# A router in plain fp32, and a final norm in which the gain is multiplied ahead of the factor

## What is computed

```python
x = x + concatenate([a, r]) @ w_out[l]
h = rmsnorm(x, ffn_norm[l])                   # x / sqrt(mean(x^2) + eps) * gain
logits = h @ w_router                         # 256 x 8
top_logits, top_idx = lax.top_k(logits, 2)
gates = softmax(top_logits)
x = x + sum over the 2 experts e of  gate_e * ((silu(h @ w_gate[e]) * (h @ w_up[e])) @ w_down[e])
return rmsnorm(x, final_norm)
```

## Time and profile before

| what | value |
|---|---|
| median of 3 runs | 1946.05 us (1945.35 to 1947.36) |
| the profiled execution | 1945.6 us, span 1943.3 us |
| TensorE busy | 1894.8 us, 98% of the span |
| VectorE busy | 1499.3 us, 77% |
| ScalarE busy | 1239.7 us, 64% |
| GpSimd busy | 391.1 us, 20% |
| granted TensorE clock, mean | 0.993 of full speed |
| expert stage | from about 976 to 1928 us |

### The profile page before, as it was taken

One profiled execution on the slowest core, in us unless ns is written; L12 is line 12 of the kernel. 1 busy time (PEld: TensorE's weight loads), 2 busy tenths in 40 slices (PEclk: granted clock), 3 DMA queues, 4 the chain that ended last, 5 costly groups with the idle time before them and its releaser, 6 DMA issues.

```text
span 1943.3 us, 27184 instructions
## 1 busy us (share of the span) xinstructions
PE 1894.8 (98%) x9931; PEld 1611.9 (83%) x9931; DVE 1499.3 (77%) x1604; ACT 1239.7 (64%) x1441; POOL 391.1 (20%) x204
## 2 busy tenths in 40 slices
PE   8999999999998999999899999999999999999997
PEld 6788879998887999878688888888888888888885
DVE  7545356666765666696689999999999999899997
ACT  6554444444643444464378888888878888888885
POOL 6756870001823000282340000000000000000000
PEclk9999999999999999999999999999999999999999
DMA  9534556665433667443489999999999999999994
GB/s 277 171 111 131 177 172 207 224 217 163 138 120 108 209 214 227 152 138 124 147 332 394 376 396 378 375 395 354 395 355 397 396 354 395 355 395 396 357 396 177
DMA packets 251401, 524.54 MB, mean 270 GB/s; under 512 B 10008, under 2 KB 58784, under 8 KB 251184
## 3 DMA queue, kind: packets, MB, share of 16 engines
q1 hardware_dynamic: 244000, 506.36, 73.1%
q10 hardware_dynamic: 5088, 10.03, 1.4%
q0 software_dynamic: 2224, 6.96, 1.1%
HBM read 508.12 MB, written 15.20 MB: 269 GB/s over the span
## 4 chain that ended last, share of the span: by engine, by line
PE 89%; DVE 6%; ACT 2%; issue 2%; DMA 0%; POOL 0%; DVEq 0%; SPq 0%; ACTq 0%
PE bank L696 27%; PE bank L698 26%; PE bank L697 26%; PE bank L1048 1%; PE bank L1214 1%; DVE w_lo_sb L1781 1%; PE bank L770 1%; PE bank L743 1%; PE bank L749 1%; ACT w_hi_sb L1351 0%; DVE left_hi_sb L1740 0%; PE bank L1101 0%; ACT w_hi_sb L1371 0%; DVE arena L1736 0%; PE bank L1099 0%
## 5 line engine op out<-in xcount | busy, mean ns | idle before, releaser
L1781 DVE TENSOR_TENSOR w_lo_sb<-arena,w_hi_sb 128x1024 fp32r<-128x1024 f32 x672 | 806.6, 1223 | 74.7 <-ACT w_hi_sb L1351 48.9
L1351 ACT ACTIVATE w_hi_sb<-arena 128x1024 fp32r<-128x1024 f32 x672 | 710.3, 1062 | 165.3 <-PE bank L698 164.7
L696 PE MATMUL bank<-w_hi_sb,left_hi_sb 128*128 128x512 f32 (+1 forms) x1424 | 563.4, 396 | 9.6 <-POOL w_lo_sb L632 3.8
L698 PE MATMUL bank<-w_hi_sb,left_lo_sb 128*128 128x512 f32 (+1 forms) x1424 | 552.2, 388 | 0.0
L697 PE MATMUL bank<-w_lo_sb,left_hi_sb 128*128 128x512 f32 (+1 forms) x1424 | 551.4, 387 | 0.0
L1371 ACT ACTIVATE w_hi_sb<-arena 128x1024 fp32r<-128x1024 f32 (+1 forms) x269 | 280.3, 1052 | 351.7 <-PE bank L698 338.8
L632 POOL TENSOR_TENSOR w_lo_sb<-arena,w_hi_sb 128x1024 fp32r<-128x1024 f32 (+1 forms) x134 | 341.6, 2566 | 579.5 <-ACT w_hi_sb L1371 579.0
L696 PEld LDWEIGHTS bank<-w_hi_sb,left_hi_sb 128*128 128x128 f32 x1424 | 268.0, 188 | 68.7 <-POOL w_lo_sb L632 9.4
L698 PEld LDWEIGHTS bank<-w_hi_sb,left_lo_sb 128*128 128x128 f32 x1424 | 267.8, 188 | 55.9
L697 PEld LDWEIGHTS bank<-w_lo_sb,left_hi_sb 128*128 128x128 f32 x1424 | 268.3, 188 | 52.1 <-issue 0.7
L1793 DVE TENSOR_TENSOR w_lo_sb<-arena,w_hi_sb 128x1024 fp32r<-128x1024 f32 x135 | 163.6, 1219 | 126.3 <-ACT w_hi_sb L1371 125.3
(11 more groups left out here) (327 smaller groups left out, 1620.8 us busy)
## 6 DMA issues: line engine op xcount, KB each, us to landing
arena<-in_moe_w_gate SPq DMA_DIRECT2D x112, 1024.0 KB, 7.5
arena<-in_moe_w_up SPq DMA_DIRECT2D x112, 1024.0 KB, 8.1
arena<-in_moe_w_down SPq DMA_DIRECT2D x112, 1024.0 KB, 7.5
arena<-in_w_in SPq DMA_DIRECT2D x45, 1024.0 KB, 5.1
arena<-in_w_ffn_in SPq DMA_DIRECT2D x22, 1024.0 KB, 6.1
arena<-in_w_out SPq DMA_DIRECT2D x12, 1024.0 KB, 5.0
arena<-in_w_ffn_out SPq DMA_DIRECT2D x11, 1024.0 KB, 4.8
arena<-in_dense_w_gate SPq DMA_DIRECT2D x11, 1024.0 KB, 5.9
```

The costliest lines, as they stand in the source:

```text
L696: pe.matmul(out, still[0], moving[0], start=start, stop=False)
L698: return pe.matmul(out, still[1], moving[0], start=False, stop=stop)
L1351: act.activation(expert_buffer(w_hi_sb, j), expert_piece(j % MOE_SUBS), ACT.Copy) \
L1781: dve.tensor_tensor(expert_buffer(w_lo_sb, j), expert_piece(j % MOE_SUBS), expert_buffer(w_hi_sb, j).bitcast(F32), ALU.subtract) \
```

## The change

Four things change. The router's product is done in plain fp32: VectorE writes each turned bank once, multiplied by the gain, into `router_x`, and TensorE multiplies it by the unsplit router weights, one `matmul` for each k; the splits of the router weights go. Of the final norm, ScalarE sums the squares by halves of a tile, each half as soon as it is added. VectorE multiplies x by the gain ahead of the mean, into `gained`. The factor is then applied to tile 0 on VectorE and to tile 1 on ScalarE, with a semaphore each for SyncE. And ScalarE's read of the rounds moves from behind the experts to between expert 1 and the loop over experts 2 to 6.

```diff
-        router_hi_sb, router_lo_sb = (sb(f"router_{n}_sb", KD * EXPERTS, F32R) for n in ("hi", "lo"))
...
+        router_x = tiles(work(11264, KD * TOKENS), KD)
         e_back = [h, tiles(work(8192, T * D))]
+        gained = e_back[1]
...
             for t in range(T):
-                sp.wait_ge(sem("result"), t + 1)
+                sp.wait_ge(sem(f"result{t}"), 1)
                 sp.dma_start(out.rearrange("a (t p) d -> p (a t) d", p=P)[:, t, :], x[:, t, :]) \
                     .then_inc(sem("stored"), 16)
...
-                mm = three_passes(b[0:EXPERTS, 0:TOKENS],
-                                  [a[:, k * EXPERTS:(k + 1) * EXPERTS] for a in (router_hi_sb, router_lo_sb)],
-                                  (left_hi[:, k, :], left_lo[:, k, :]), k == 0, k == KD - 1)
+                mm = pe.matmul(b[0:EXPERTS, 0:TOKENS], router_w[:, k, :], router_x[:, k, :],
+                               start=(k == 0), stop=(k == KD - 1))
...
                 expert(0, True, False)
                 expert(1, True, False, lambda: copy_y(0, None))
+                act.wait_ge(sem("rounds_known"), 1)
+                rounds = act.value_load(e_rounds[0:1, 0:1], min_val=1, max_val=MAX_ROUNDS)
                 with act.Fori(2, LAST) as e:
                     expert(e, True, False, lambda: copy_y(e - 1, e * 16 - 16))
                 expert(LAST, False, True, lambda: copy_y(LAST - 1, LAST * 16 - 16))
+                return rounds
...
-            first_round()
-            act.wait_ge(sem("rounds_known"), 1)
-            rounds = act.value_load(e_rounds[0:1, 0:1], min_val=1, max_val=MAX_ROUNDS)
+            rounds = first_round()
...
             act.activation(root, ones[:, 0:T], ACT.Sqrt)
             for t in range(T):
-
-                act.wait_ge(sem("e_added"), rounds * (4 * EXPERTS) + (4 - 2 * T + 2 * (t + 1)))
-                act.activation(h[:, t, :], x[:, t, :], ACT.Square, accum_out=ss[:, t:t + 1]) \
-                    .then_inc(sem("ss_last"), 1)
-                act.wait_ge(sem("ss_last"), told("ss_last"))
+                for half in range(2):
+                    act.wait_ge(sem("e_added"), rounds * (4 * EXPERTS) + (2 * t + half + 1))
+                    cols = slice(half * 512, (half + 1) * 512)
+                    act.activation(h[:, t, cols], x[:, t, cols], ACT.Square, accum_out=ss[:, half * T + t:half * T + t + 1]) \
+                        .then_inc(sem("ss_last"), 1)
             act.wait_ge(sem("ms_ready"), norm_number["last"])
             act.activation(root, ms, ACT.Sqrt).then_inc(sem("root_ready"), 1)
+            act.wait_ge(sem("rinv_ready"), norm_number["last"])
+            act.activation(x[:, 1, :], gained[:, 1, :], ACT.Identity, scale=rinv[:, 1:2]).then_inc(sem("result1"), 1)
...
-            flat_w = router_w[:, :, :].rearrange("p k e -> p (k e)")
-            link(dve.tensor_copy(router_hi_sb[:, :], flat_w))
-            link(dve.tensor_tensor(router_lo_sb[:, :], flat_w, router_hi_sb[:, :].bitcast(F32), ALU.subtract))
...
-                    split_out(f"hT_{tag}", gain_T[tag], range(2 * half, 2 * half + 2),
-                              freed=span[f"wo{suffix}.1.{4 * half}"][1])
+                    turned = range(2 * half, 2 * half + 2)
+                    if tag != "g1":
+                        split_out(f"hT_{tag}", gain_T[tag], turned, freed=span[f"wo{suffix}.1.{4 * half}"][1])
+                        continue
+                    dve.wait_ge(sem("w_used"), span[f"wo{suffix}.1.{4 * half}"][1])
+                    for i in turned:
+                        k = slice(2 * i, 2 * i + 2)
+                        mul(router_x[:, k, :], tiles(bank_of("hT_g1", i)[:, :], 2), over(gain_T["g1"][:, k], 2, TOKENS),
+                            "pair_read")
...
-            dve.wait_ge(sem("ss_last"), T)
-            mean(ms, ss[:, 0:T], D, "ms_ready")
-            factor("last")
             dve.wait_ge(sem("final_gain_landed"), 16)
             for t in range(T):
-                dve.scalar_tensor_tensor(x[:, t, :], x[:, t, :], rinv[:, t:t + 1], fin_gain, ALU.mult, ALU.mult) \
-                    .then_inc(sem("result"), 1)
+                mul(gained[:, t, :], x[:, t, :], fin_gain, "last_gained")
+            mean_square("last")
+            factor("last")
+            dve.tensor_scalar(x[:, 0, :], gained[:, 0, :], rinv[:, 0:1], None, ALU.mult).then_inc(sem("result0"), 1)
```

## The result

The changed kernel takes 1949.14 us (median of 21 runs); the kernel before took 1946.08 in 21 runs beside it. The ratio is 1.0014, 95% interval 1.0008 to 1.002: 2.7 us slower (1.6 to 3.9), within the 0.2% that I called no change.

The account below looks back on a forecast made before the run. TensorE was taken to bound the kernel, so time changes only where it waits, around the router and behind its last product. 0 - 0.15 + 0 + 2.25 = +2.1 on 1946.05 gives 1948.15 us, range 1945.2 to 1950.2.

Parts of the forecast that it names:

- The splits of the router weights: Dropping VectorE's two splits of the router weights gains 0, since VectorE later idles 1.99 us for TensorE; at most 2 us.
- The router: At the router, fp32 matmuls replace three passes; the logits' copy comes 0.24 us sooner, bounds 0.1 and 0.4, behind ScalarE's root.
- Half of it through the clock: At the gather behind the router, run mostly at the lower clock, half of the copy's gain gets through: -0.15 us.
- rival D: Between router and expert 0 the clock behaves differently: 1945.55 us with a faster gather, or up to 1949.65; chance 0.10.
- ScalarE's read: Moved between expert 1 and 2, ScalarE's read of the rounds takes 1.3 us; under 1.65 us it costs nothing: 0.
- rival C: ScalarE's moved read is long and stops TensorE: 1949.25 us at a 2.73 us read, 1950.4 at 3.91; chance 0.14.
- The final norm: At the kernel's end, gain products ahead of the factor make tile 0 ready at R + 4.27 instead of R + 2.0: +2.25 us.
- R: The time VectorE comes out of its read and branch behind the last residual, ahead of the final norm; taken as 1936.82 us.
- rival B: At the final norm VectorE was free at 1933, waiting for ScalarE, so the products hide under the squares: 1944.75 us; chance 0.08.
- rival A: At the final norm VectorE leaves its branch sooner, at ScalarE's 2.73 us, R 1.2 us less: +0.9, 1946.95 us; chance 0.13.
- The first store sets the end: The two tiles' stores go back to back, 1.3 us each, so the end moves with tile 0.

Follow-up runs that it names:

- e9: e8 with two of ScalarE's four splits of the first expert's weights moved behind the router norm's root; 1942.68 us, ratio 0.9978 to the kernel before.
- e11: The kernel before with only the router in fp32, and two of ScalarE's four splits moved behind the root; 1945.43 us, ratio 0.9991.
- e10: e8 with the router part of the change taken back; 1945.48 us, ratio 0.9987 to the kernel before.
- e2: The changed kernel with the router part taken back, leaving the final norm and ScalarE's moved read; 1949.21 us, ratio 1.0009 to the kernel before.
- e3: The changed kernel with VectorE's read of the rounds moved ahead of its expert loop; 1946.84 us, ratio 1.0001 to the kernel before.
- e4: The changed kernel without the second round's body and branch on any engine, VectorE's read still at the end; 1944.57 us, ratio 0.9987.
- e6: e3 with the final norm written twice, first where one round reaches it without a jump, again behind the second round's body; 1944.3 us, ratio 0.9991.
- e7: e3 with factor and gain again in one instruction, both tiles on VectorE; 1948.57 us, ratio 0.9997 to the kernel before.
- e8: e7 with e6's order, the final norm ahead of the second round's body; 1944.73 us, ratio 0.9993 to the kernel before.

## Why the prediction was right

The forecast was 1948.15 us, +2.1; measured are 1949.14 and +2.7 by the ratio (+3.1 by the medians), no change by the bound of 0.2%. By its steps:

- **The splits of the router weights, 0.** The traces bear this out. From the copy ahead of the splits to the first product that waits for TensorE behind them it was 6.78 us before (97.80 to 104.58) and 6.81 after. Without the splits the two products between took 2.85 us in place of 1.42, and VectorE idled 2.51 in place of 1.99. Before, then after:

```profile
97.80 1.42 DVE L1736 COPY arena<-bank 128x512 f32<-128x512 f32 x2 [1.93 <-PE bank L770]
```

```profile
100.42 1.42 DVE L1739 COPY arena<-bank 128x512 f32<-128x512 f32 x2 [1.94 <-PE bank L771]
101.87 2.85 DVE L1743 TENSOR_TENSOR arena<-arena 128x512 f32<-128x512 f32 x2
107.23 0.69 DVE L1743 TENSOR_TENSOR arena<-bank,const_sb 128x512 f32<-128x512 f32 x1 [2.51 <-PE bank L837]
```

- **The router, copy 0.24 sooner, bounds 0.1 to 0.4.** It was 0.18 (6.42 to 6.24), behind a reciprocal that waits for the root, as the step says. The estimate of 0.45 us for a matmul measured 0.47 (1.89 for four). TensorE had the logits 5.08 us behind the second residual add for 6.31 before, 1.23 sooner where the step has 1.6: the matmuls began 0.3 us later than I took, and ran 0.1 longer. None of this reached the copy, as forecast; VectorE stood 1.78 us for the root, and e9 and e11 got 1.05 back. I had named the stall without asking what it would take to remove it.
- **Half of it through the clock, -0.15.** This can't be read: the gather took 5.75 us instead of 6.45, 0.70 less, but it took 5.16 to 6.71 in the other kernels, with 5.16 and 6.71 both under the old router (e10, e2). The granted clock explains the size: in the changed kernel it is at 0.50 from 972 to 978 and at 1.00 again from 979 on, so the last quarter of the gather ran at the upper level. This is rival D's place. Its effect is there, but with the root in its old place the ranges overlap, 5.3 to 6.7 with the new router and 5.2 to 6.7 with the old, so no part of it can be put down to the change.
- **ScalarE's read, 0.** Right, and rival C is out. Behind the experts the read was 0.85 us of idle time where I took 1.3, and 1.65 was the point from which it would cost. But the step had it stand in ScalarE's way and be made up for by the buffers. Here nothing had to be made up for: from 1208.46 to 1222.61 before and from 1212.43 to 1226.58 after, ScalarE did the same in the same 14.15 us, hole for hole. From expert 0's first product to the start of the last residual add it is 953.9 to 954.2 us in all fourteen kernels, so VectorE's moved read cost the expert stage nothing either. The Trainium skill ("Runtime: NRT & Kernel Launch", instruction fetch mechanics) says that a taken branch to a page that isn't at hand waits for a DMA to fetch it. The runs agree: the branch has 3.0 of VectorE's 4.0 us and 1.9 of ScalarE's 2.75, instruction packets move there, and it costs at most 0.13 us when the code that follows stands next to it.
- **The final norm, +2.25.** Tile 0 moved by 2.33 (5.92 to 8.25). The mechanism is the one forecast: the products start at R, 2.1 us behind ScalarE's last square, so rival B is out. From R it was 4.17 us where I had 4.27 (the tensor_scalar of 1024 columns took 0.75, my 0.8). R itself was 0.17 later than the row of before, and 0.12 earlier in e2, so that is scatter; rival A, R 1.2 us sooner, is out, and e3 and e4 show why the engines differ: VectorE's branch costs 1.1 us more than ScalarE's.
- **The first store sets the end.** The two tiles still went back to back, but from tile 0 to the end of the span it took 5.00 us for 4.47. I had this at 0. It was 4.4 to 4.5 in six of the fourteen kernels and 4.8 to 5.5 in the others; the bulk of the data takes some 2.6 us at about 400 GB/s in all. Before and then after, with the DMA engines' busy share and GB/s in the last two columns:

```profile
1942.00:1942.50 0.50, 0.00 (x0) 0.00 (x0) 0.00 (x0) 0.00 (x0) 0.00 (x0) 0.50 0.69 270
1942.50:1943.00 0.50, 0.00 (x0) 0.00 (x0) 0.00 (x0) 0.00 (x0) 0.00 (x0) 0.50 0.00 0
```

```profile
1946.60:1947.10 0.50, 0.00 (x0) 0.00 (x0) 0.00 (x0) 0.00 (x0) 0.00 (x0) 0.50 1.01 393
...
1948.60:1949.10 0.50, 0.00 (x0) 0.00 (x0) 0.00 (x0) 0.00 (x0) 0.00 (x0) 0.50 0.09 33
1949.10:1949.60 0.50, 0.00 (x0) 0.00 (x0) 0.00 (x0) 0.00 (x0) 0.00 (x0) 0.50 0.00 0
1949.60:1950.10 0.50, 0.00 (x0) 0.00 (x0) 0.00 (x0) 0.00 (x0) 0.00 (x0) 0.50 0.00 0
```

  The difference is in a few late packets, the 33 GB/s of 1948.6 to 1949.1. In windows of 0.1 us the last packets move 3.6 to 3.7 us behind tile 0 in the six kernels and 3.9 to 4.7 in the eight; from there to the end of the span, in which nothing moves, it is 0.7 to 1.0 us in all. What sets the eight apart is in the DMA queues too: between tile 0 and the end they have 1 to 4 packets of kind "instruction" beside the 288 of the stores (one in after, e2 and e3, at 1947.5 to 1948.0 in after), and the six have none. So instruction fetches under the stores go with the longer end in fourteen of fourteen; that they are its cause no run shows by itself.

By the trace the sum is 2.33 + 0.53 - 0.18 = +2.7 us without the gather, which is what the ratio says. With the gather's 0.70 it is +2.0, and that is what these two executions differ by from the second residual add to the end (987.26 us for 985.31). So the norm and the copy were sized within 0.1 us, the missing term is the 0.53 at the stores, and the -0.15 of the gather is not shown. That the forecast's +2.1 lies so near this +2.0 is luck: the missing 0.53 and the gather's further 0.55 cancel.

The profiled execution lies 6.3 us above that of before, and 4.85 of it are there already at the second residual add (962.84 for 957.99), where both kernels have done the same work but for two small splits. In part that comes from one wait of TensorE for GpSimd's low parts. Before, and after:

```profile
54.37 0.80 PE L696 MATMUL bank<-w_hi_sb,left_hi_sb 128*128 128x512 f32 x1 [2.74 <-POOL w_lo_sb L632]
```

```profile
56.51 0.80 PE L697 MATMUL bank<-w_hi_sb,left_hi_sb 128*128 128x512 f32 x1 [4.73 <-POOL w_lo_sb L633]
```

The second residual add stood between 956.7 and 962.8 us over the fourteen kernels, with 956.86 and 962.42 in two that differ only behind the experts (e6, e7). So this is scatter of single executions, which would also explain why the intervals are 3 us wide.

## What to carry over

Before work is moved ahead of a factor, read when its engine gets there: here VectorE came out of a read and a branch later than the sums it was to overlap with, so 2.5 us of new products stood wholly on the path, and even with the branch gone they were longer than the last square they could hide behind. An idle stretch that the profile puts down to "issue" behind a conditional is worth one experiment that moves the likely path in front of the skipped body; here the first tile came 2.2 us (e7 to e8) and 2.9 us (e3 to e6) sooner. The jump isn't free where it now falls: with it under the stores the end was 0.4 to 1.0 us longer than in the kernel before. And an edit that makes one input of a join sooner is worth little until the other is looked at: the fp32 router alone gave 0.18 us, with the root two splits earlier 1.24, and by the rows of before the root alone would have given nothing.

## What the hardware showed that I had not expected

- A condition whose body is long cost 3.0 us on VectorE and 1.9 on ScalarE when it was skipped, and at most 0.13 us when the code that ran stood right behind it (e3, e4, e6). Instruction packets moved on the DMA queues there, and none in the kernel without the body.
- Reading one number from SBUF into a register behind the last work took 1.0 us on VectorE and 0.85 on ScalarE, nearly as much as a split of 128 x 1024 (1.06); between two of ScalarE's splits it left no idle time at all.
- A gather of 32 records took from 5.16 to 6.71 us under the same instructions, by when within it the granted clock came back from 0.50 to 1.00.
- From the first tile's readiness to the end of the span it took 4.4 to 5.5 us for the same 1.05 MB: at most 4.5 in the six kernels without an instruction packet under the stores, 4.8 and more in the eight with one.
